# RMS-norm sums in a hybrid decoder step: one more GpSimd add per norm, one TensorE product less

## What is computed

```python
def rmsnorm(x, g):
    xf = x.astype(jnp.float32)
    var = jnp.mean(xf * xf, axis=-1, keepdims=True)
    return (xf * lax.rsqrt(var + NORM_EPS)).astype(x.dtype) * g
...
for i in range(DEPTH):
    xn = rmsnorm(h, W['norm_mix'][i])
    ...                                   # mixer of the layer, added to h
    hn = rmsnorm(h, W['norm_mlp'][i])
    h = h + jnp.square(jax.nn.relu(hn @ W['mlp_w_up'][i])) @ W['mlp_w_down'][i]
    gate = jax.nn.sigmoid(rmsnorm(h, W['norm_ple'][i]) @ W['ple_w_gate'][i])
    h = h + (p[i] @ W['ple_w_proj'][i]) * gate
y = rmsnorm(h, W['norm_final'])
```

## Time and profile before

| | |
|---|---|
| median of 3 runs | 2058.88 us |
| lowest and highest | 2054.94 and 2062.57 us |
| the profiled execution | 2062.73 us, span 2061.1 us |
| TensorE products busy | 1832.2 us, 89% |
| VectorE busy | 1338.7 us, 65% |
| ScalarE busy | 937.4 us, 45% |
| GpSimd busy | 519.8 us, 25% |

### The profile page before, as it was taken

How to read it: one execution, slowest core, us unless ns; L and a number is a source line. 1 busy time by engine, 2 the same in 40 slices (tenths; PEclk the granted TensorE clock), 3 DMA queues, 4 the chain that set the end, 5 groups by cost and what they waited for, 6 DMA issues and landing times.

```text
span 2061.1 us, 35718 instructions
## 1 busy us (share of the span) xinstructions
PE 1832.2 (89%) x13417; PEld 1665.7 (81%) x13417; DVE 1338.7 (65%) x2464; ACT 937.4 (45%) x1677; POOL 519.8 (25%) x427
## 2 busy tenths in 40 slices
PE   4999989999989328999999859999899998999996
PEld 4898759999989103399999849999889875899996
DVE  5998796555476884255556866554699879665544
ACT  2555654453334771145433444543345567445332
POOL 2500501441130232234212104421331041044112
PEclk9999989999999558999999979999999998899998
DMA  5454483655556797945554506555445348465540
GB/s 179 124 183 134 114 262 115 208 182 165 168 204 221 261 375 274 356 147 180 169 165 143 171 14 216 181 183 173 137 130 184 113 118 262 148 193 184 174 152 22
DMA packets 317968, 365.02 MB, mean 177 GB/s; under 512 B 7802, under 2 KB 290978, under 8 KB 317750
## 3 DMA queue, kind: packets, MB, share of 16 engines
q1 hardware_dynamic: 296068, 287.41, 44.6%
q0 software_dynamic: 20560, 74.62, 9.8%
q10 hardware_dynamic: 1216, 1.35, 0.2%
HBM read 340.79 MB, written 23.15 MB: 177 GB/s over the span
## 4 chain that ended last, share of the span: by engine, by line
PE 64%; DVE 21%; ACT 6%; issue 3%; DVEq 3%; DMA 1%; POOLq 1%; POOL 0%; ACTq 0%; SPq 0%
PE G L525 18%; PE G L526 17%; PE G L527 17%; DVE wlo L1516 5%; PE A L831 3%; ACT whi L971 3%; DVE sums L1832 2%; DVE pg L1893 2%; DVE pg L1891 2%; PE A L491 1%; DVE xbc L1687 1%; DVE xL L1577 1%; DVE xg L1567 1%; DVEq L1689 1%; DVE stx L1824 1%
## 5 line engine op out<-in xcount | busy, mean ns | idle before, releaser
L1516 DVE TENSOR_TENSOR wlo<-raw,whi 128x2048 fp32r<-128x2048 f32 x234 | 545.8, 2333 | 358.8 <-ACT whi L971 358.7
L971 ACT ACTIVATE whi<-raw 128x2048 fp32r<-128x2048 f32 x234 | 447.9, 1914 | 591.6 <-PE G L527 587.5
L525 PE MATMUL G<-xH,whi 128*128 128x264 f32 x2112 | 610.6, 289 | 45.5 <-DVE xL L1577 29.1
L526 PE MATMUL G<-xH,wlo 128*128 128x264 f32 x2112 | 603.6, 286 | 0.0
L527 PE MATMUL G<-xL,whi 128*128 128x264 f32 x2112 | 603.1, 286 | 0.0
L525 PEld LDWEIGHTS G<-xH,whi 128*128 128x128 f32 x2112 | 403.1, 191 | 55.3 <-issue 24.2
L526 PEld LDWEIGHTS G<-xH,wlo 128*128 128x128 f32 x2112 | 403.4, 191 | 0.3
L527 PEld LDWEIGHTS G<-xL,whi 128*128 128x128 f32 x2112 | 401.4, 190 | 0.0
L525 PE MATMUL G<-aH,whi 128*128 128x264 f32 x1024 | 292.9, 286 | 8.3 <-DVE wlo L1516 8.3
L526 PE MATMUL G<-aH,wlo 128*128 128x264 f32 x1024 | 291.5, 285 | 0.0
L527 PE MATMUL G<-aL,whi 128*128 128x264 f32 x1024 | 291.5, 285 | 0.0
(11 more groups left out here) (404 smaller groups left out, 3124.8 us busy)
## 6 DMA issues: line engine op xcount, KB each, us to landing
raw<-in_mlp_w_up SPq DMA_DIRECT2D x64, 1024.0 KB, 5.4
raw<-in_mlp_w_down SPq DMA_DIRECT2D x64, 1024.0 KB, 5.1
raw<-in_ssd_w_in SPq DMA_DIRECT2D x48, 1024.0 KB, 5.4
pg<-in_cache_k POOLq DMA_DIRECT2D x64, 512.0 KB, 5.6
pg<-in_cache_v POOLq DMA_DIRECT2D x40, 512.0 KB, 6.2
raw<-in_ssd_w_out SPq DMA_DIRECT2D x16, 1024.0 KB, 7.3
raw<-in_ple_w_gate SPq DMA_DIRECT2D x16, 1024.0 KB, 5.1
raw<-in_moba_w_qkv SPq DMA_DIRECT2D x12, 1024.0 KB, 5.1
```

What stands on the lines that cost most here:

```text
L525: mm(o, whi[u % 2][:, k, w], act_h[:, x, :], start=first, stop=False)
L526: mm(o, wlo[u % 2][:, k, w], act_h[:, x, :], start=False, stop=False)
L971: fn(whi[u % 2][:], raw[(u + 2) % 4][:], ACT.Copy).then_inc(s_hi, 1)
L1516: V.tensor_tensor(wlo[u % 2][:], raw[(u + 2) % 4][:], whi[u % 2][:].bitcast(F32), ALU.subtract).then_inc(s_lo, 1)
```

## The change

`squares` adds the two halves of `ssq` into the first half of `hh2` at its end (128x264, the new L1361), with a drain ahead of it, and signals `s_ssq` from there. `norm_sum` does one product, with that half, in place of two.

```diff
@@ def norm_sum(n):
                 pe.wait_ge(s_ssq, n + 1)
-                mm(bank[0][:, 0:T], ones[:], ssq[:, 0, :], start=True, stop=False)
-                mm(bank[0][:, 0:T], ones[:], ssq[:, 1, :], start=False, stop=True).then_inc(s_var, 1)
+                mm(bank[0][:, 0:T], ones[:], hh2[:, 0, :], start=True, stop=True).then_inc(s_var, 1)
@@ def squares(n):
                     gp.tensor_tensor(hh2, hr, hr, ALU.mult)
                     pool.drain()
-                    f = gp.tensor_tensor(ssq, ssq, hh2, ALU.add)
-                    if r < 3:
-                        pool.drain()
-                f.then_inc(s_ssq, 1)
+                    gp.tensor_tensor(ssq, ssq, hh2, ALU.add)
+                    pool.drain()
+                gp.tensor_tensor(hh2[:, 0, :], ssq[:, 0, :], ssq[:, 1, :], ALU.add).then_inc(s_ssq, 1)
```

## The result

| | before | after |
|---|---|---|
| median of the runs, us | 2059.71 (22 runs, 2054.94 to 2063.33) | 2062.52 (22 runs, 2057.36 to 2067.38) |
| ratio after / before | | 1.0017, 95% interval 1.0009 to 1.0025 |
| profiled execution, its time and span, us | 2062.73, 2061.1 | 2067.12, 2065.1 |

The change costs 3.5 us (0.0017 x 2060; interval 1.9 to 5.2). The profiled execution is one of the slower ones of its kernel (22 runs, the second highest), so distances inside it are read here, not its end.

A forecast was written before the change was run, and what follows sets the result against it. It took TensorE, with 64% of the chain, to bound the kernel, norm products being on the path at n = 1, 4, 7, 10, 11, 12. Terms -0.85 + 0.0 + 0.9 + 0.0 = +0.05 us gave 2058.9 us, range 2054.5 to 2064.5.

The forecast's parts named there:

- What an add costs: GpSimd's new 128x264 add: 0.76 us alone, between 0.61 and 1.29, and 0.68 us once `wlo` has ended.
- When it may run: At norms beside VectorE's `wlo`: the add is held off until `wlo` ends, some 2.7 us long, TensorE idle 0.1 to 0.4 us.
- The step that decides: GpSimd's add against VectorE's `wlo`: whichever runs first holds the other off until it has ended.
- The up norms and the gate: Norms n = 1, 4, 10, 11 save 0.10 us each and n = 7 saves 0.45: -0.85 us in all.
- The final norm: n = 12: drain and add cost 0.14 + 0.76 us on GpSimd, TensorE saves 0.88: 0.0 us.
- The load at n = 0: `cst` behind the add, some 1.2 us late, covered by TensorE's spare time: 0 us, bounds 0 and +2.4.
- The load at n = 9: `cst` about 2.9 us late in layer 3, one stretch at half clock behind the pause: +0.9 us, bounds 0 and +2.6.
- The late state load: Rival, 20%: TensorE pauses at n = 9 and n = 0 bring slow stretches, 2.6 + 2.4 us; +4.15 in all, 2063.0 us.
- The free gain: Rival, 12%: the add overlaps `wlo`, five norms save 0.45 us each, `cst` lateness is hidden: -2.25 us, 2056.6 us.
- every product on the path: Rival, 3%: removed products count at all norms, 12 x 0.45 + 0.88 = 6.3 us less, 2052.6 us.
- slow stretches after every short wait: Rival, 3%: each new TensorE wait is followed by a stretch at half clock: +11.6 less 0.45, about 2070.0 us.
- the forecast case: Whole kernel: between -1.5 and +1.5 us around no change, 62%.

The follow-up runs named there:

- e7: Changed kernel with the change undone at n = 0 and n = 9, where loads stand behind the add: 2058.49 us, 0.9992 of the kernel before.
- e4: Changed kernel with SyncE's weight load for group 5 of layer 3's xbc stage held until `cst` has landed: 2057.51 us, 0.9995 of the kernel before.
- e5: Changed kernel with the halves of `ssq` folded after the third row block and two 128x264 adds after the fourth: 2053.85 us, 0.9971 of the kernel before.
- e6: Changed kernel with the new add, its result unread, and the two products of before: 2068.5 us, 1.0037 of the kernel before.
- e9: The same kernel as e5, changed kernel with the earlier fold, timed on another occasion: 2056.06 us, 0.9979 of the kernel before.
- e1: Kernel before with the new add and the one product at n = 9 alone: 2064.3 us, 1.0023 of the kernel before.
- e8: Changed kernel with 11 unread products put ahead of TensorE's wait for `cst` in layer 3: 2062.39 us, 1.0016 of the kernel before.
- e2: Changed kernel with the loads `cst` and `wdt` issued ahead of the new add: 2059.03 us, 0.9991 of the kernel before.
- e3: Kernel before without the second product of each norm and with no add in its place: 2056.5 us, 0.9988 of the kernel before.

## Why the prediction was nearly right, and where it was not

**What an add costs** (0.76 alone, 0.68 after release): measured 0.74 and 0.62. Right. The Trainium skill (GPSIMD Engine Reference, 3.1, Elementwise) gave an estimate of 0.57 us; by 0.74 us for 264 columns and 1.29 us for 528 the cost here, an estimate from these two, is 2.1 ns a column and 0.19 us besides, and the measurement decides.

**When it may run.** Predicted: 2.7 us long at n = 1, 2, 4, 5, 8, 10 and 11, L495 late there by 0.1 to 0.4 us, not at n = 3, 6, 7. Measured: 2.62 us, and L495 0.19 to 0.23 us late at just these seven (0.31 to 0.35 us behind the product ahead of it, instead of 0.12), not at the three. Idle time of TensorE in the records is less than the 0.1 to 0.4 us that were to be seen, 31 to 69 ns. The add is 2.62 us long at n = 3, 6, 7 and 9 too; there TensorE comes later. The step that decides was right.

**The up norms and the gate** (-0.10 at each of four, -0.45 at n = 7, sum -0.85). From the last product of group 0 to the first of group 1 the changed kernel saves 0.11, 0.11, 0.12 and 0.13 us at n = 1, 4, 10 and 11, and 0.45 at n = 7, together 0.92. Right at all five. The way from one L495 to the next is no measure of it: n = 7 to 8 takes 191.79 us against 192.06, which looks like 0.27 instead of 0.45, but it ends at the L495 of n = 8, which is itself 0.23 us late (191.55 + 0.23 = 191.78). Timed (e7), -1.7 us with zero in reach of the interval; the term can't be told from it.

**The final norm** (0.0). From the start of the last 128x528 add to that of the root: 3.52 us before, 3.51 after (2046.52 to 2050.03). Right.

**The load at n = 0** (0, bounds 0 and +2.4): +0.6 in the distance. TensorE waits 1.35 us for `cst` and runs at half clock behind it for 6.8 us instead of 3.4, but most of that is hidden. The length of the wait doesn't decide: in e4 it is 1.86 us and in e5 1.80, with 3.4 us at half clock, and the distance is 31.21 and 31.20, as before. The distance is longer only in the traces with 6.8 us at half clock behind the wait: 31.82 here, 32.16 in e6, 33.03 in e9.

**The load at n = 9** (+0.9, bounds 0 and +2.6): +6.3 us in the changed kernel's trace, +4.7 in the one with this part alone, timed +4.7. **This is the term that failed, and by its size it is the whole miss.** In the prediction's words, `cst` "goes out about 2.9 us later and lands at 1495.65", and TensorE "idles about 3.2 us". The 2.7 us of delay were there. What failed is that the transfer was moved and its duration of 5.15 us kept. The delay brought it from 2.4 us ahead of SyncE's 1 MB weight load (1487.60 and 1489.98 before) to 0.4 us behind it, and beside that it takes 8.0 us (7.7 to 8.0 in e1, e6 and e8, which have the same order, and 4.8 to 5.1 in e2, e4, e5 and e7, where it leads or the weight load is held back). The prediction moved GpSimd's queue and never put SyncE's timeline beside it. Nearly the whole lengthening stands ahead of its first piece. The wait was then 5.96 us instead of 3.2; the slow stretches were two or three instead of one; and VectorE's slack, which was to hide a shift of 2.9 us, was used up: it waits 4.00 us. With the delay alone (weight load held back) the distance grew by 0.55 us: that part of the working stands.

The Trainium skill says (DMA: Bandwidth & Descriptors, Queues, rings and completion order) that each DMA engine goes round between the queue rows it has work for, packet by packet. The traces agree in direction only: a small load pays for a large one queued on another row. They show no turn after each piece. In the changed kernel nothing of `cst` starts in the 3.4 us (1488.18 to 1491.58) in which 938 KB of the weight load do. How many pieces make one packet in the Trainium skill's sense, and so whether this is its rule or something else, the profile doesn't show; the cause of the holding back stays open.

**The rivals.** The late state load (20%, 2063.0 us) is what happened, in place and nearly in sum (measured 2062.5): with only n = 9 of its two places, and there 4.7 to 6.3 us instead of 2.6. That the sums are so close is luck: n = 9 cost about twice its price and n = 0 next to nothing of its 2.4 us. The free gain is excluded by the 2.62 us of the add, every product on the path by the -2.5 us of e3 (-4.5 at most), and slow stretches after every short wait by e7, which has those waits and was not slower. The range held since it reached to this rival; the forecast case did not.

## What to carry to other kernels

An operation added ahead of a DMA issue costs what the issue loses, not what the operation takes: here a 0.74 us add held a load back for 2.7 us, since it had to sit out a VectorE subtraction, and the delay put that load behind another one, which held it for 2.8 us more. When a transfer moves, move it against every other queue's timeline and ask what it will now travel beside; its duration from the old trace holds only if that stays the same. An engine that waits should do its folding while it waits: the same sum, folded one row block earlier, had the single product without the late load at n = 9.

## What the hardware showed that was not expected

- At n = 9 a load of 24x4096 fp32 took 4.8 to 5.1 us when it left ahead of a 1 MB load of another queue or without it, and 7.7 to 8.0 us when it left 0.4 us behind it. (At n = 0, with no weight load near, it took 5.4 to 5.7 us.) In the slow case its first piece starts 3.9 to 4.1 us after the issue instead of 1.2, when over 0.9 MB of the other load have started.
- TensorE's clock came back late: after a pause of 5.96 us it was at 0.50 (1.2 GHz of 2.4) for 10.2 us, though the engine worked again from 1495.54 on, 0.8 us after the clock had fallen at 1494.7. After a pause of 5.68 us (e1) it was 6.8 us, after one of 5.51 us (e6) 10.2 us again, so the pause's length alone doesn't decide. Unread products in the pause kept it at 1.00 up to 1499 us and gave 2.8 us back at this place in the trace, though not in the timed total.
- Slow stretches of 3.4 us also come and go, between executions, at places the edits don't touch. Each is worth up to 1.7 us, as much as most terms of this prediction, and the total time of a single execution can't tell such terms apart.
